# First mixer: 16x16 solves per lane with 32x32 block products, opening and low-rank stage in one, column turns in quarters

## What is computed

```python
def _rwkv7_step(S, inp):                      # 256 steps, 16 heads, S is 64 x 64
    r_t, w_t, k_t, v_t, a_t, b_t = inp
    sa = jnp.einsum('bhij,bhj->bhi', S, a_t)
    S = S * w_t[:, :, None, :] + sa[..., None] * b_t[:, :, None, :] + v_t[..., None] * k_t[:, :, None, :]
    y = jnp.einsum('bhij,bhj->bhi', S, r_t)
    return S, y

r, k, v = jnp.einsum('pbtd,pde->pbte', xs[:3], w_rkv)
w = -jax.nn.softplus(-(w0 + jnp.tanh(xw @ w1) @ w2)) - 0.5
a = jax.nn.sigmoid(a0 + (xa @ a1) @ a2)
g = jax.nn.sigmoid(xg @ g1) @ g2
...
bonus = jnp.sum(rh * kh * r_k.astype(f32), -1, keepdims=True) * vh
out = (yn + bonus.reshape(B, T, D)).astype(h.dtype) * g
```

## Time and profile before

| | us |
|---|---|
| median of three runs | 1409.67 |
| the profiled execution | 1406.89 |
| its span | 1405.2 |
| TensorE matmuls busy | 1320.7 (94%) |
| VectorE busy | 906.8 (65%) |
| ScalarE busy | 672.0 (48%) |
| GpSimd busy | 218.3 (16%) |

### The profile page before, as it was taken

One profiled execution on the slowest core, in us unless ns is written; L12 is line 12 of the kernel. 1 busy time (PEld: TensorE's weight loads), 2 busy tenths in 40 slices (PEclk: granted clock), 3 DMA queues, 4 the chain that ended last, 5 costly groups with the idle time before them and its releaser, 6 DMA issues. The chain is left out here.

```text
span 1405.2 us, 19630 instructions
## 1 busy us (share of the span) xinstructions
PE 1320.7 (94%) x7848; PEld 1074.9 (76%) x7848; DVE 906.8 (65%) x1255; ACT 672.0 (48%) x968; POOL 218.3 (16%) x123
## 2 busy tenths in 40 slices
PE   6998889999999989899999989989999989989998
PEld 2784558678888786677888868978887878868987
DVE  1687895778778667668665474655455587554664
ACT  2544343264443355555443345655563767436561
POOL 0001551131000040304000001200001342500300
PEclk9999998999999989999999999999999999999999
DMA  8861560539889664367675449715543531038840
GB/s 313 308 205 49 179 242 2 194 128 319 282 298 310 219 193 169 132 202 232 225 241 182 148 117 207 223 50 158 186 143 107 184 133 61 32 101 169 213 148 30
DMA packets 160635, 247.24 MB, mean 176 GB/s; under 512 B 15064, under 2 KB 100028, under 8 KB 160032
## 3 DMA queue, kind: packets, MB, share of 16 engines
q1 hardware_dynamic: 159216, 239.61, 53.7%
q0 software_dynamic: 1328, 6.38, 1.2%
HBM read 244.86 MB, written 4.24 MB: 177 GB/s over the span
## 5 line engine op out<-in xcount | busy, mean ns | idle before, releaser
L199 DVE TENSOR_TENSOR w_lo<-w_raw,w_hi 128x2048 fp32r<-128x2048 f32 (+3 forms) x176 | 402.6, 2295 | 240.0 <-ACT w_hi L190 239.9
L217 PE MATMUL ps<-w_hi,act_hi 128*128 128x512 f32 (+4 forms) x1216 | 472.6, 389 | 16.1 <-DVE act_lo L877 6.4
L219 PE MATMUL ps<-w_hi,act_lo 128*128 128x512 f32 (+4 forms) x1216 | 462.8, 381 | 0.0
L218 PE MATMUL ps<-w_lo,act_hi 128*128 128x512 f32 (+4 forms) x1216 | 462.5, 380 | 0.0
L190 ACT CAST w_hi<-w_raw 128x2048 fp32r<-128x2048 f32 (+3 forms) x176 | 316.8, 1806 | 248.3 <-PE ps L219 206.9
L217 PEld LDWEIGHTS ps<-w_hi,act_hi 128*128 128x128 f32 x1216 | 230.8, 190 | 62.3 <-issue 15.6
L219 PEld LDWEIGHTS ps<-w_hi,act_lo 128*128 128x128 f32 x1216 | 230.3, 189 | 37.2
L218 PEld LDWEIGHTS ps<-w_lo,act_hi 128*128 128x128 f32 x1216 | 230.8, 190 | 34.4 <-issue 1.0
L684 POOL TENSOR_TENSOR nstat<-nstat,con 128x1 f32<-128x1 f32 x8 | 5.4, 680 | 416.9 <-DVE nstat L679 416.9
L217 PE MATMUL ps<-w_hi,ffn_gh 128*128 128x512 f32 x176 | 69.7, 396 | 0.0
L219 PE MATMUL ps<-w_hi,ffn_gl 128*128 128x512 f32 x176 | 68.6, 390 | 0.0
(11 more groups left out here) (516 smaller groups left out, 1734.2 us busy)
## 6 DMA issues: line engine op xcount, KB each, us to landing
w_raw<-in_ffn_w_in SPq DMA_DIRECT2D x88, 512.0 KB, 4.8
w_raw<-in_fox_w_in SPq DMA_DIRECT2D x32, 912.0 KB, 8.3
w_raw<-in_ada_w SPq DMA_DIRECT2D x28, 1024.0 KB, 5.9
w_raw<-in_ffn_w_out SPq DMA_DIRECT2D x20, 1024.0 KB, 5.4
w_raw<-in_rwkv_w_rkv SPq DMA_DIRECT2D x12, 1024.0 KB, 7.0
con<-in_ada_w SPq DMA_DIRECT2D x48, 256.0 KB, 5.2
w_raw<-in_gla_w_in SPq DMA_DIRECT2D x10, 896.0 KB, 4.7
w_raw<-in_gdn_w_in SPq DMA_DIRECT2D x10, 896.0 KB, 4.9
```

The costliest lines, as they stand in the source:

```text
L199: self.nc.vector.tensor_tensor(lo[:, s, 0:c["nk"], 0:c["width"]], self.raw[:, c["slot"], 0:c["nk"], 0:c["width"]], hi[:, s, 0:c["nk"], 0:c ...
L217: nc.tensor.matmul(out(t)[:, 0:w], xh[:, k, tok], hi[:, s, j, 0:w], start=start, stop=False)
L218: nc.tensor.matmul(out(t)[:, 0:w], xh[:, k, tok], lo[:, s, j, 0:w], start=False, stop=False)
L219: return nc.tensor.matmul(out(t)[:, 0:w], xl[:, k, tok], hi[:, s, j, 0:w], start=False, stop=stop)
```

## The change

- Products with one moving column (ada turns, the decay across a tile, the same in the linear mixer) are made in four column groups of 32 instead of one of 128.
- `rwkv_low` is gone: its work stands in `rwkv_open`. The down products and the up products of a run between the last two weight chunks, the rest after the last; the w2 and a2 loads are issued after chunk 9 is used, those of g2 and r_k after chunk 11. The gate's up products follow the running sums at once. The bonus row and its sum move there from `rwkv_mid`.
- In `rwkv_mid` the across products stand after the first turns, ada items after units 8 and 12 of the b grams, units 6 and 10 of the k grams, after level 4, and at the end.
- Each lane inverts two 16x16 blocks in 15 steps of two instructions. A level 4 (16 to 32) is added as products of 32x32 blocks (`turn4`, `ax4`, `xax4`), level 5 turns only diagonal blocks (`turn5`), and all levels go in two groups of 16 tile-heads. The keep-warm products after `turn_up(0)` go.
- GpSimd clears the place of the inverses at unit 8, and its two products with gate and norm rows wait for the inverses.

```diff
-    def column_halves(self, out, lhs, right, start=True, stop=True):
+    def column_halves(self, out, lhs, right, start=True, stop=True, n=64):
-        for c in (0, 64):
-            r = self.nc.tensor.matmul(out[c:c + 64], lhs[:, c:c + 64], right, start=start, stop=stop)
+        for c in range(0, P, n):
+            r = self.nc.tensor.matmul(out[c:c + n], lhs[:, c:c + n], right, start=start, stop=stop)
         return r
+    def column_quarters(self, out, lhs, right, start=True, stop=True):
+        return self.column_halves(out, lhs, right, start, stop, 32)
...
@@ stage_rwkv_open: sync
+            core.issue(sp, chunks[-1]["g"] + 1)
+            sp.wait_ge(core.used, used(len(chunks) - NSPL))
+            sp.dma_start(w2[0:64, :], a["rwkv_w2"][0]).then_inc(sem("w2"), 16)
...
             core.issue(sp, chunks[-1]["g"] + 1 + NRAW)
+            sp.wait_ge(core.used, used(len(chunks) - 1))
+            sp.dma_start(g2[:, 0, :], a["rwkv_g2"][0, 0:P]).then_inc(sem("g2"), 16)
...
@@ tensor
+            def rates(i):
+                if i:
+                    return
+                pe.wait_ge(sem("low_w"), 48)
+                pe.wait_ge(sem("xs"), 5 * KD)
...
+                ups(0, a2, (0, 1, 4, 5))
+                for k in range(KD):
+                    r = nc.tensor.matmul(ps[0:32, 7, 0:T], g1[:, k, P:160], gate_in[:, k, :], start=(k == 0), stop=(k == KD - 1))
+                r.then_inc(sem("down"), 1)
...
+            ups(1, w2, (6, 0, 1, 4))
...
+            cum(0)
...
+            cum(1)
+            pe.wait_ge(sem("g2"), 32)
+            pe.wait_ge(sem("exps"), 3)
...
@@ vector
+            def rates(n):
+                if n == len(chunks) - 2:
+                    mixed(3)
+                if n == len(chunks) - 1:
+                    mix(core, dve, sem, 3, dx, h, decay_in)
+                    mix(core, dve, sem, 5, dx, h, gate_in)
+                    keys()
...
+            keyed(0)
+            keyed(1)
+            dve.wait_ge(core.used, used(len(chunks) - 1))
...
+            scaled(0)
+            scaled(1)
@@ stage_rwkv_mid: tensor
+            def blocks(t, out, lhs, right, done, rows=range(4)):
+                for j in range(H64):
+                    for c in rows:
+                        s = slice(32 * c, 32 * c + 32)
+                        r = nc.tensor.matmul(out(j, s), lhs(H64 * t + j, s), right(H64 * t + j, s), start=True, stop=True)
+                r.then_inc(sem(done), 1)
...
+            def ax4(t):
+                pe.wait_ge(sem("low4"), t + 1)
+                blocks(t, lambda j, s: ps[s, 2 + 2 * t, 16 * j:16 * j + 16], lambda th, s: gram[s, th, s], lambda th, s: mm.low4[s, th, :], "ax4")
...
+            turn4(0)
+            turn4(1)
+            ax4(0)
+            ax4(1)
+            xax4(0)
+            xax4(1)
+            item()
+            turn5(0)
+            turn5(1)
             ax5(0)
-            turn_up(2)
             ax5(1)
             xax5(0)
-            turn_up(3)
             xax5(1)
             ax6(0)
             ax6(1)
             xax6(0)
             xax6(1)
-            ax5(2)
-            ax5(3)
-            pe.wait_ge(sem("low"), 4)
             sa(0)
             sa(1)
...
@@ gpsimd
-                if u == 10:
-                    pool.wait_ge(sem("kv"), KD)
+                if u == KD:
+                    pool.wait_ge(sem("k_grams"), KD)
                     nc.gpsimd.memset(up[:, :, :], 0.0).then_inc(sem("blank"), 1)
...
+            pool.wait_ge(sem("up_back"), 4)
             pool.wait_ge(sem("bvg"), 2)
@@ vector
-            for j in range(31):
-                n, c = 31 - j, j + 1
-                part = mm.tmp[:, 0:n * c].rearrange("p (r c) -> p r c", c=c)
+            lt16, inv16 = diagonal16(lt), diagonal16(inv)
+            for j in range(15):
+                n, c = 15 - j, j + 1
+                part = mm.tmp[:, 0:2 * n * c].rearrange("p (m r c) -> p m r c", m=2, c=c)
...
+            def level4(t):
+                dve.wait_ge(sem("up4_mm"), t + 1)
+                for b in range(0, P, 32):
+                    v.tensor_copy(up[b:b + 16, H64 * t:H64 * t + H64, b + 16:b + 32], heads16(3 + 2 * t)[b:b + 16]).then_inc(sem("up4"), 1)
```

More of the change, by code:

```diff
@@ new lines, in sides @@
+            def sides(t, bank, first, lhs, right, done):
+                for j in range(H64):
+                    side = slice(64 * ((j + first) % 2), 64 * ((j + first) % 2) + 64)
+                    r = nc.tensor.matmul(ps[side, bank, 64 * (j // 2):64 * (j // 2) + 64], lhs(H64 * t + j), right(H64 * t + j), start=True, stop=True)
+                r.then_inc(sem(done), 1)
+            left = lambda s: slice(s.start, s.start + 16)
+            right_ = lambda s: slice(s.start + 16, s.start + 32)
@@ L1862, in blocks64 @@
-            def blocks64(q, bank, lhs, right, done):
-                for j in range(8):
-                    side = slice(64 * (j % 2), 64 * (j % 2) + 64)
-                    r = nc.tensor.matmul(ps[side, bank, 64 * j:64 * j + 64], lhs(8 * q + j, j), right(8 * q + j, j), start=True, stop=True)
-                r.then_inc(sem(done), 1)
-            def ax6(q):
-                pe.wait_ge(sem("low5"), q + 1)
-                blocks64(q, 3 + 2 * (q % 2), lambda th, j: gram[0:64, th, 64:P], lambda th, j: low[0:64, th, 0:64], "ax6")
@@ new lines, in xax4, with turn5, ax5 @@
+            def xax4(t):
+                pe.wait_ge(sem("x4"), t + 1)
+                blocks(t, lambda j, s: ps[left(s), 3 + 2 * t, 16 * j:16 * j + 16], lambda th, s: mm.x4[s, th, :], lambda th, s: up[s, th, right_(s)], "up4_mm")
+            def turn5(t):
+                pe.wait_ge(sem("up4"), 4 * t + 4)
+                blocks(t, lambda j, s: ps[s, t, 32 * j:32 * j + 32], lambda th, s: up[s, th, s], lambda th, s: core.c("ident")[s, s], "turn5", range(3))
+            def ax5(t):
+                pe.wait_ge(sem("low"), 2 * t + 1)
+                pairs(t, lambda j, even, odd: ps[odd, 2 + 2 * t, 32 * j:32 * j + 32], lambda th, even, odd: gram[even, th, odd],
+                      lambda th, even, odd: low[even, th, 0:32], "ax5")
@@ new lines, in ax6, with xax6 @@
+            def ax6(t):
+                if t == 0:
+                    pe.wait_ge(sem("low_blank"), 1)
+                pe.wait_ge(sem("low5"), t + 1)
+                sides(t, 3 + 2 * t, 1, lambda th: gram[0:64, th, 64:P], lambda th: low[0:64, th, :], "ax6")
+            def xax6(t):
+                pe.wait_ge(sem("x6"), 2 * t + 2)
+                pe.wait_ge(sem("up5"), 2 * t + 2)
+                sides(t, 2 + 2 * t, 0, lambda th: mm.x6[64:P, th, :], lambda th: up[64:P, th, 64:P], "up6_mm")
@@ L2067, in _ @@
             square(3)
-            ada.act_part(act, sem, held)
+            item()
         @block.gpsimd
```

516 lines of the change are left out of this document (237 added, 279 removed).

## The result

The changed kernel takes 1419.22 us (median of 4 runs, 1418.78 to 1421.05); the kernel before took 1409.42 (1402.44 to 1409.72) in the same comparison. The ratio is 1.0094, 95% interval 1.0074 to 1.0114 (the two medians alone give 1.0070; one of the four runs before lies 7 us under the others): slower by some 0.9%, above the range forecast. The profiled execution took 1418.78 us, its span 1416.8.

What follows compares the result with a forecast made beforehand. TensorE was taken as 94% busy over 1405.2 us, the first mixer as five stretches with different limits. Terms 1.5+2.5+5.1+14.8-18.4 = 5.5 us gained gave 1401.4 profiled, 1404.2 as median; range 1387 to 1417.

Steps and rivals of the forecast that it cites:

- Column turns, in the opening: Two turns before the first tokens fall from 3.4 us to 1.0 or 2.0; gain 1.5 us, bounds 0 and 2.4.
- Merged opening: Opening and low-rank stage merged: the next stage, turns and grams, starts 5.1 us earlier, bounds 3 and 6.
- Grams: Turns and grams on TensorE, with two ada items and the across columns added: 24.6 us against 22.7.
- Perhaps 0.7 waiting for a transfer: Gram stage: possible TensorE wait of 0.7 us for a weight transfer, named with the ada items added there.
- Solve and transposes: VectorE's solve takes 10.7 us for 27.4; the transposes before and after it stay at 7.9 and 8.0.
- Cover fails: Rival, 13%: TensorE's work ends after the solve, or the merged stage ends no earlier; 3 to 5 us, 1408.
- Doublings: From turned inverses to VectorE's first rhs addition: 49.5 us where 31.1 stood, a loss of 18.4.
- the array, the bank or the supply of tiny instructions: Rival, 15%: four blocks do not overlap in turn4, ax4, xax4, turn5; 31 ns a record, +15 us, 1420.
- Clock: Doubling chain: low clock, granted near 0.5, from about the turned inverses until sa.
- Bank rule: Second rival's ground, for four row groups: different row tiles cannot use one PSUM bank at once; no-overlap chance 15%.
- Behind the mixer: Column quarters in the 80 records outside the first mixer: 2.5 us gained, bounds 0 and 7.

Runs made afterwards that it cites:

- old_mid: Merged opening and column quarters of the changed kernel, with the gram, solve and doubling stage of the kernel before, less its bonus work: ratio 0.9922 to the kernel before.
- merge_only: As old_mid, but column turns and sums are whole 128-column products again everywhere: ratio 0.996 to the kernel before.
- warm_end: Changed kernel with six 512-wide identity products on TensorE at the end of the opening: ratio 1.01 to the kernel before.
- items_back: Changed kernel with its first two ada items moved out of the turns and grams to beside the key grams: ratio 1.0067 to the kernel before.
- padded: Changed kernel with one 512-wide identity product after each of the first five groups of level 4: ratio 1.0074 to the kernel before.
- halves_turn: Changed kernel with level-4 and level-5 turns as one product per 64 rows, 64-column weights, in place of two of 32: ratio 1.0091 to the kernel before.
- item_early: Changed kernel with the ada item between levels 4 and 5 moved beside the key grams, before turn4: ratio 1.0086 to the kernel before.
- warm_chain: Changed kernel with three 512-wide identity products between the last kv product and turn4: ratio 1.0095 to the kernel before.
- quarters_only: Kernel before with only its column turns and the linear mixer's sums in four 32-column products each: ratio 0.9979 to the kernel before.
- filled: As items_back, with the ada item from between levels 4 and 5 moved between the two ax4 groups: ratio 1.0068 to the kernel before.
- old_mid_warm: old_mid with two 512-wide identity products at the end of the opening: ratio 0.991 to the kernel before.

## Why the prediction was wrong

Two steps failed, the gram stage with two ada items in it (11.2 us up to T) and the pace of the doublings (7.2 us after it); the other rows of the table above add up to 1.4 us the other way. Part by part:

**Column turns, in the opening.** Right. The two turns take 1.3 us from 18.25 on, where 3.4 stood. Timeline of TensorE, changed kernel:

```profile
18.25 0.56 PE L212 MATMUL ps<-con,ada_part 128*32 128x1 f32 x32
19.18 0.43 PE L212 MATMUL ps<-con,ada_part 128*32 128x1 f32 x32 [0.37 <-ACT ada_part L352]
19.55 1.09 PE L1465 MATMUL ps<-con,x_res 128*128 128x128 f32 x8
```

The second turn takes 0.37 us to the next start, 12 ns a record, between the bounds of 8 and 16. Not all of the difference is the quarters' doing: the eight token turns behind them took 1.09 us here and 1.95 before, so TensorE ran at another pace, though the granted clock reads 1.00 in both profiles.

```profile
21.92 1.95 PE L1445 MATMUL ps<-con,x_res 128*128 128x128 f32 x8
```

At the faster pace, 110 ns a record, the old turns would have taken some 1.8 us (an estimate). What they bring depends on the rest: 0.4 us at the start of the gram stage alone, 2.1 on top of the merge (140.0 in old_mid, 142.1 in merge_only); I had 1.5.

**Merged opening.** Forecast 5.1, bounds 3 to 6; merge_only gives 3.8 up to the stage's start and 5.6 us by its ratio. Right, a little large. What I left out is that its last 2.7 us are idle on TensorE, and that the clock falls there. That cost 3.8 us up to the first mask and 1.7 at the end of the gram stage (warm_end).

**Grams: the first step that failed,** 36.2 us for 24.6. "Perhaps 0.7 waiting for a transfer" was 4.7 us of waiting and a stage held up around it. The item was priced by TensorE's 2.3 us (two of them and 1.5 for the across columns are the 6.1 of the sum, which the 0.7 did not enter); its other price is 2 MB of weights that can be asked for only when a slot is free. I had counted three chunks loaded ahead and two per item, and not done the subtraction. items_back took this and the second low stretch of the clock (0.56 in 168.3 to 172.2) away: 52.6 us from the stage's start to T for the forecast's 51.2. There the stage alone took 25.5 us without the items, more than the 24.6 forecast with them; with the items' 4.5 and the wait's 4.7 that is 34.7 of the 36.2 (an estimate).

**Solve and transposes.** 10.2 us for 10.7, transposes 8.1 and 7.9. Right. "Cover fails" did not happen in the form it was named: TensorE's kv products ended at 198.7, ahead of T at 202.1, in the changed kernel. With the items moved (items_back) turn4 waited 1.0 us beyond T for ScalarE's copy of them. But the solve had covered transfers too. In its 27.4 us the DMA engines were busy 0.85 of the time; the new one leaves 10.2 us, and the loads go on before it (into the grams) or after it (into the doublings).

**Doublings: the second step that failed.** Sizes in the order of the sum, forecast and measured: turn4, ax4 and xax4 11.0 less 1.0, 19.6; item 4.2, 4.0; turn5 4.0, 2.4; ax5 4.0, 8.3; xax5 8.0, 5.1; ax6 and xax6 8.2, 6.9; sa to the addition 11.1, 10.4. The array's terms were all somewhat too large (level 4 without its gaps 9.0 us: four groups of 1.7 and two of 1.08). Two were far too small, and both contain gaps. The forecast took "the array, the bank or the supply of tiny instructions" as one rival with 15%, at 31 ns a record; level 4 came to 19.6 us / 768 = 26 ns, above the 23 from which that rival decides, and the kernel is slower, as it said. That its total, 1420, is nearly what was measured is chance: it had put 15 us on this chain, which came to 7 us over the forecast, and the other 11 came from the grams. What held the records back is the last of its three causes: padded shows that the array had room, and halves_turn, item_early and warm_end (gap behind record 112 of each group, 12 records having been added ahead) that the gap follows the place in the instruction stream.

The page had the means to see it. Level 4 is 1536 instructions, all short; the chain before had 5 fetches of 16 KB in 31 us and none of them showed as a gap (the earlier trace rows lie in it): there 256 instructions took 6 us, longer than a fetch.

**Clock.** Right: 0.52 to 0.73 from T to sa. The Trainium skill, "TensorE: Matmul & The Clock Gate", Part 1, with the rule that activity releases the clock, is not contradicted by the changed kernel: in level 4 TensorE was busy 9.85 of 19.7 us. I read the fall as one that small products cause even when dense, and padded speaks for that and against the rule: its TensorE had no idle time from 202.94 to 221.9 and still ran at 0.50 up to 219.4, with 0.91 from there to 222.6. By the measurement activity alone did not release the clock there; what did at 219.4 is open. Windows of padded:

```profile
218.30:219.40 1.10, 1.10 (x129) 1.10 (x128) 0.00 (x0) 0.00 (x0) 0.00 (x0) 0.50 0.00 0
219.40:222.60 3.20, 2.61 (x148) 1.68 (x135) 1.68 (x4) 0.00 (x0) 0.00 (x0) 0.91 0.02 5
```

**Bank rule.** The forecast named the Trainium skill, "TensorEngine Tiling (Array Packing)", Gotcha 1, by which different row tiles cannot use one PSUM bank at the same time. Four row groups wrote one bank in turn4, at 8.5 ns a record at full clock (warm_chain) and 13 at the low one (padded), where I had 8 and 16 for a loss-free overlap. No run here shows a cost of it.

**Behind the mixer.** 4.6 us for 2.5, and 5.6 in quarters_only and 6.4 in old_mid, counted from the first state-fed addition: the term was too small, within its bounds of 0 and 7. That quarters_only gains only 3.0 us in the whole is its slower gram stage; why its clock fell there was not tried.

**What was inferred and what was shown.** That the gap is a wait for instructions is shown by padding that costs nothing and by the gap's place in the stream. That a fetch takes longer under weight loads is borne out by the long gaps (4.2 to 5.2 us for some 2), which stood where loads filled the DMA engines: ax5's fell from 4.78 to 1.52 us when the item's loads were moved away (item_early), and xax4's grew from 2.67 to 5.18 when they were moved there (filled). What exactly delays it was not tried. The Trainium skill, "DMA: Bandwidth & Descriptors", section "Queues, rings and completion order", says that each DMA engine takes turns between queues packet by packet, the instruction refill among them, which would fit. The Trainium skill, "Runtime: NRT & Kernel Launch", section "Instruction fetch mechanics", gives the 16 KB block of 256 instructions, as seen here, but says that crossing a block's end is mostly hidden; here the measurement decides otherwise, with 3.45 to 4.0 us a block as the pace and up to 5.2 us of gap.

## What to carry to other kernels

Price a chain of small products twice, by the array and by its instruction count, and take the larger: here a block of 256 TensorE instructions (128 fp32 records) cost at least 3.45 us, and up to 4.0 with idle DMA engines, 27 to 31 ns a record, and a few long products placed into such a stretch were free. When a long step is shortened, ask what transfers it covered as well as what work; and an item that streams weights costs the slot and the transfer of its next chunk, which is due a stage later and may land in a stretch that lives on instruction fetches. The parts that paid here, the merged opening and the column quarters, gave 0.78% with the old solve (old_mid's interval is 0.5 to 1.0%), and are the version to keep (old_mid).

## What the runs showed of the hardware that I had not expected

- A stretch of dense small products stalls for its own instructions: one gap of 1.6 to 2.7 us per 256 instructions with idle DMA engines, 4.2 to 5.2 us under full weight loads.
- Small products on four row and column groups cost 8.5 ns a record at the full clock and 13 at the low one (32-column weights). Products with 64-column weights in two groups cost 53 at the low one (halves_turn): half as many records took twice as long.
- Behind an idle stretch of 2.4 to 2.7 us of TensorE at a stage's end the granted clock was 0.50, and the way to the first mask was 3.8 us longer where column sums and turns stood there (warm_end, 4.7 for 8.5 us) and 1.2 where turns alone did (old_mid_warm, 3.95 for 5.18). In quarters_only it fell behind 0.93 us of idle time, where the kernel before, with the same 0.93, kept 1.00: the length of the idle stretch alone does not decide it.
